# Rows turned for the router ahead of their norm, the norm's weight folded into the router matrix, and tile 0 placed one PSUM bank at a time

## The chip, the cores and the metric

The kernel runs on one core of one Trainium2 chip, in one launch. The metric is the device time of that launch in microseconds. It is a hybrid block of a network (a mixer of three branches, then a mixture of experts) in float32, written directly for the five engines, with every wait on a semaphore in the code.

## The reference

512 tokens of width 1024. What matters here is what follows the mixer:

```python
xn = rms_norm(x, norm1_g[l])
x = x + hybrid_mixer(xn, ...)            # ends with: merged @ w_out
xn = rms_norm(x, norm2_g[l])             # x * rsqrt(mean(x*x) + 1e-6) * g
x = x + hierarchical_moe(xn, ...)
...
return rms_norm(x, final_norm_g)

def hierarchical_moe(x, wg, bg, we, be, w_gate, w_up, w_down):
    g_logits = xt @ wg + bg              # 4 groups
    g_idx = argmax(g_logits)
    e_logits = (xt @ we + be) of the chosen group   # 4 of 16 experts
    top_p, top_i = lax.top_k(softmax(e_logits), 2)
    combine = g_w * top_p / sum(top_p)   # on the two experts chosen
    for e in range(16):
        h = silu(xt @ w_gate[e]) * (xt @ w_up[e])
        y = y + combine[:, e:e + 1] * (h @ w_down[e])
```

## The kernel before, in words

**Two-part arithmetic.** Every large product is made of three matmuls: each operand is split into a high part (ScalarE writes `w_hi`, `xT_hi`, ... as fp32r) and the rest (`w_lo`, `xT_lo`, ..., a subtraction on GpSimd or VectorE). A weight block is 128x1024 elements, 512 KB. Blocks are numbered `b`; four slots (`HI_SLOTS`) hold split blocks. `split_hi(b)` waits until TensorE is done with block `b - 4`; TensorE waits for `split_lo(b)` with `lo_wait`. On SyncE's queue the loads of the next blocks wait for `lo_wait` of the block whose buffer they take.

**The end of the mixer.** `merged @ w_out` is made in two column halves. The first half is four blocks (`B_OUT` to `B_OUT + 3`, 24 matmuls each). The second half, blocks `B_OUT + 4` to `B_OUT + 7`, goes by rows: for each of four row tiles `t` the 24 matmuls of all four blocks, so that row tile 0 is ready first. After a row tile (`x2_ps`) VectorE adds the residual (`x_rows`, semaphore `x2_done`), ScalarE squares and sums the row (`y_tile`, `x2_sq`), VectorE scales the sum, GpSimd takes the power -1/2 (`stat`), VectorE writes the normed rows `xn2`. TensorE turns `xn2` in eight transposes (`turn_xn2`), ScalarE copies the turned rows out of PSUM (`xn2T`), and TensorE multiplies them with the 20 columns of `router_w` (`logits`).

The loop on ScalarE which serves this part is the same before and after the change. Its order is what counts: the square of row tile `t` stands ahead of the copy of row tile `t - 1`.

```python
for t in range(NT + 1):
    if t < NT:
        act.wait_ge(S["x2_done"], NT + t + 1)
        ...activation(y_tile, x_rows[:, t, :], ACT.Square, ...)
    if 1 <= t <= NT:
        act.wait_ge(S["xn2T_ps"], t)
        ...activation(xn2T[:, (t - 1) % 2, :], ps[...], ACT.Copy)
```

Just ahead of that loop ScalarE splits the four blocks of the second half. Between `split_hi(B_OUT + 3)` and `split_hi(B_OUT + 4)` it issues six small loads on its own queue, among them the router matrix (`route_in`, `g2_in`).

**Routing.** VectorE turns the logits into two experts for each token in a chain of small operations on `route` (each `link` waits for the one before), gives TensorE the choice in bf16 (`picked`), which counts tokens per expert with triangular matrices, and computes a slot of the scratch table `slots` for each token. Tile 0 (the first 128 tokens of expert 0) is not read back from `slots`: VectorE writes a 0/1 matrix into `silu` (`tile0_where`) and TensorE places the rows with 32 float32 matmuls into two PSUM banks (`ps[:, 3:5]`). In the meantime GpSimd scatters `xn2` into `slots` with eight indirect DMAs (`scattered`), from which SyncE loads the rows of tiles 1, 2 and so on.

**Expert tiles.** A tile is twelve blocks: eight for gate and up, four for down of the tile before. 14 tiles stand in fixed order, the others come from a table. `on_pool` says which `split_lo` GpSimd makes: of the expert blocks only the first four of tile 0. `AHEAD = 3`: splits run three blocks ahead of TensorE. At the end GpSimd gathers the results from `slots` and VectorE weighs and norms them.

Of the kernel before, what the change touches and what calls it, by code (L numbers as in the profile page):

```python
# [26 lines left out]
ALU = mybir.AluOpType  # L27
# [54 lines left out]
def on_pool(r):  # L82

    return r < 4

LO_DVE_0 = 32


def pool_before(r):
    return sum(on_pool(x) for x in range(r))


def build(nc, a, out):
# [10 lines left out]
    with ctx:  # L106
# [70 lines left out]
        with ExitStack() as s2:  # L177
# [15 lines left out]
            sb(s2, "to_line", [P, 8])  # L193
# [32 lines left out]
        def y_hi(t):  # L226
# [16 lines left out]
            "tile0_where xn2T_ps xn2T_done logits_ps gexp_in gexp_done eexp_done picked counts_ps routed scattered tab "  # L243
# [61 lines left out]
        POOL_TILE = pool_before(8 + PER_TILE) - pool_before(8)  # L305
        DVE_TILE = PER_TILE - POOL_TILE

        def lo_wait(eng, b):

            if b < B_EXP:  # L310
                eng.wait_ge(S["lo_pool"], b + 1)
            elif on_pool(b - B_EXP):
                eng.wait_ge(S["lo_pool"], B_EXP + pool_before(b - B_EXP + 1))
            else:
                eng.wait_ge(S["lo_dve"], LO_DVE_0 + b - B_EXP + 1 - pool_before(b - B_EXP + 1))

        def lo_wait_loop(eng, i, r):

            tile = r // PER_TILE
            c = 8 + r % PER_TILE  # L320
            if on_pool(c):
                eng.wait_ge(S["lo_pool"], i * POOL_TILE + (B_EXP + pool_before(c + 1) + (tile - 1) * POOL_TILE))
            else:
                eng.wait_ge(S["lo_dve"],
                            i * DVE_TILE + (LO_DVE_0 + c + 1 - pool_before(c + 1) + (tile - 1) * DVE_TILE))
# [15 lines left out]
        def split_lo(eng, b):  # L341
# [4 lines left out]
               .then_inc(S["lo_pool"] if b < B_EXP or on_pool(b - B_EXP) else S["lo_dve"], 1)  # L346

        def split_lo_loop(eng, at, r):
# [3 lines left out]
               .then_inc(S["lo_pool"] if on_pool(8 + r) else S["lo_dve"], 1)  # L352
# [11 lines left out]
        def _(sp):  # L364
# [119 lines left out]
            for r in range(PER_TILE):  # L484
                if r == 3:

                    sp.wait_ge(S["scattered"], 16 * 2 * NT)
# [31 lines left out]
        def _(pool):  # L519
# [59 lines left out]
            for r in range(AHEAD):  # L579
                split_lo(pool, B_EXP + r)  # L580

# [8 lines left out]
            for r in range(AHEAD, 8 + AHEAD):  # L590
                if r < 8:
                    if on_pool(r):
                        split_lo(pool, B_EXP + r)
            for r in range(8, 8 + AHEAD):
                if on_pool(r):
                    split_lo_loop(pool, at_odd(0), r - 8)
            def tile(at):
                for r in range(PER_TILE):
# [1152 lines left out]
```

## Time and profile before

| | |
|---|---|
| Time, median of 3 runs | 869.72 us (869.38 to 871.4) |
| The profiled execution's own time | 869.15 us |
| Its span, first to last instruction | 867.4 us |
| TensorE busy | 801.0 us, 92% of the span |
| VectorE, ScalarE, GpSimd busy | 495.5, 449.2 and 218.0 us |
| Mean granted clock of TensorE | 0.965 of full |

A page of the profile gives busy times over the whole span. The change sits in some 90 us of it, so the useful views are the timelines of those stretches: each line has a start, a duration, the engine and source line, what is written from what, and in brackets how long the engine had been idle and who released it. A line with a count stands for several instructions of one kind in a row, from the first's start to the last's end. The granted clock is 1.00 for 2.4 GHz and 0.50 for 1.2 GHz.

### The profile page before, as it was taken

What the parts mean: (1) busy time and instruction counts of PE and PEld (TensorE: products, weight loads), DVE (VectorE), ACT (ScalarE), POOL (GpSimd) and SP (SyncE); (2) the same over time, 40 slices, a digit from 0 to 9 for tenths busy, and PEclk for the clock granted to TensorE, in tenths of its full rate; (3) what the DMA queues carried; (4) which work ended last, traced back from release to release, by engine and by line L of the source; (5) the groups of instructions that cost most, each with busy time, mean ns of one, the idle gap of its engine ahead of it and who ended that gap; (6) DMA issues with size and microseconds to landing.
All of it is one profiled execution on the core that took longest, in us unless ns stands there. A gap on an engine that the chain in (4) does not pass through costs nothing.

```text
span 867.4 us, 10612 instructions
## 1 busy us (share of the span) xinstructions
PE 801.0 (92%) x3635; PEld 631.7 (73%) x3635; DVE 495.5 (57%) x649; ACT 449.2 (52%) x580; POOL 218.0 (25%) x126
## 2 busy tenths in 40 slices
PE   4999999999979999999999967899999999999960
PEld 3887766676756888888888866688787787877750
DVE  6613647657472222204012435698889898988865
ACT  5244637454552232323222221687888878887842
POOL 5554323132232344444444234000000000000013
PEclk9999999999999999999999967999999999999995
DMA  8665451512120343333328364999999999975945
GB/s 308 179 243 188 128 194 49 194 49 74 40 80 27 89 169 118 99 93 95 98 96 280 131 239 197 366 400 385 405 389 393 408 395 406 389 299 209 367 137 207
DMA packets 126633, 186.76 MB, mean 215 GB/s; under 512 B 9149, under 2 KB 61957, under 8 KB 126597
## 3 DMA queue, kind: packets, MB, share of 16 engines
q1 hardware_dynamic: 119156, 167.82, 54.3%
q10 hardware_dynamic: 5136, 10.08, 3.1%
q0 software_dynamic: 2304, 8.39, 2.7%
q8 instruction: 22, 0.36, 0.2%
q14 instruction: 15, 0.11, 0.0%
HBM read 158.99 MB, written 27.28 MB: 215 GB/s over the span
## 4 chain that ended last, share of the span: by engine, by line
PE 81%; DVE 7%; ACT 4%; issue 3%; DMA 2%; POOL 1%; ACTq 1%; DVEq 0%; SPq 0%
PE ps L947 24%; PE ps L949 23%; PE ps L948 23%; PE ps L1030 3%; PE ps L1010 2%; PE ps L1171 2%; PE ps L1019 1%; DVE w_lo L350 1%; PE ps L1119 1%; ACT w_hi L339 1%; DVE rgate L1394 1%; PE ps L1178 1%; DMA x<-in_x 1%; ACT xn L879 1%; DMA slots<-y_tile 1%
## 5 line engine op out<-in xcount | busy, mean ns | idle before, releaser
L344 POOL TENSOR_TENSOR w_lo<-raw,w_hi 128x1024 fp32r<-128x1024 f32 x72 | 176.2, 2450 | 286.8 <-ACT w_hi L332 286.8
L332 ACT ACTIVATE w_hi<-raw 128x1024 fp32r<-128x1024 f32 x73 | 77.0, 1057 | 169.0 <-PE ps L949 159.9
L947 PE MATMUL ps<-xn_hi,w_hi 128*128 128x512 f32 x352 | 143.8, 409 | 0.0
L949 PE MATMUL ps<-xn_hi,w_lo 128*128 128x512 f32 x352 | 137.5, 390 | 0.0
L948 PE MATMUL ps<-xn_lo,w_hi 128*128 128x512 f32 x352 | 137.3, 390 | 0.0
L947 PE MATMUL ps<-w_hi,xT_hi 128*128 128x512 f32 x256 | 105.2, 411 | 8.1 <-DVE xT_lo L1644 5.5
L948 PE MATMUL ps<-w_lo,xT_hi 128*128 128x512 f32 x256 | 102.3, 399 | 0.0
L949 PE MATMUL ps<-w_hi,xT_lo 128*128 128x512 f32 x256 | 102.2, 399 | 0.0
L947 PEld LDWEIGHTS ps<-xn_hi,w_hi 128*128 128x128 f32 x352 | 66.0, 188 | 26.8 <-issue 13.8
L614 POOL DMA_INDIRECT raw_mg<-slots,slot_idx x7 | 6.9, 982 | 303.6 <-ACTq L930 295.1
L949 PEld LDWEIGHTS ps<-xn_hi,w_lo 128*128 128x128 f32 x352 | 66.1, 188 | 14.4
L948 PEld LDWEIGHTS ps<-xn_lo,w_hi 128*128 128x128 f32 x352 | 66.2, 188 | 13.1 <-issue 1.0
L350 DVE TENSOR_TENSOR w_lo<-raw_mg,w_hi 128x1024 fp32r<-128x1024 f32 x57 | 68.0, 1221 | 4.3 <-ACT w_hi L339 1.7
L947 PEld LDWEIGHTS ps<-w_hi,xT_hi 128*128 128x128 f32 x256 | 48.9, 191 | 24.2 <-DVE w_lo L350 8.0
L1457 DVE SCALAR_TENSOR_TENSOR macc<-raw,ps 128x512 f32<-128x512 f32 x16 | 11.0, 688 | 96.5 <-PE ps L949 96.3
L339 ACT ACTIVATE w_hi<-raw_mg 128x1024 fp32r<-128x1024 f32 x57 | 59.7, 1056 | 11.3 <-PE ps L949 11.3
L350 DVE TENSOR_TENSOR w_lo<-raw,w_hi 128x1024 fp32r<-128x1024 f32 x43 | 51.3, 1220 | 14.6 <-ACT w_hi L339 14.6
L949 PEld LDWEIGHTS ps<-w_hi,xT_lo 128*128 128x128 f32 x256 | 48.9, 191 | 11.7
L948 PEld LDWEIGHTS ps<-w_lo,xT_hi 128*128 128x128 f32 x256 | 48.9, 191 | 10.4
L947 PE MATMUL ps<-w_hi,hT_hi 128*128 128x512 f32 x128 | 51.8, 405 | 2.9 <-DVE hT_lo L1651 2.9
L339 ACT ACTIVATE w_hi<-raw 128x1024 fp32r<-128x1024 f32 x43 | 44.0, 1055 | 16.1 <-PE ps L949 16.1
L949 PE MATMUL ps<-w_hi,hT_lo 128*128 128x512 f32 x128 | 50.5, 395 | 0.0
(260 smaller groups left out, 1457.5 us busy)
## 6 DMA issues: line engine op xcount, KB each, us to landing
raw<-in_w_in SPq DMA_DIRECT2D x52, 512.0 KB, 3.7
raw_mg<-in_exp_w_down SPq DMA_DIRECT2D x36, 512.0 KB, 8.3
raw<-in_exp_w_gate SPq DMA_DIRECT2D x28, 512.0 KB, 10.3
raw_a<-in_exp_w_gate SPq DMA_DIRECT2D x27, 512.0 KB, 9.8
raw_c<-in_exp_w_up SPq DMA_DIRECT2D x27, 512.0 KB, 9.2
slots<-raw SPq DMA_DIRECT2D x24, 512.0 KB, 6.5
raw_mg<-in_exp_w_up SPq DMA_DIRECT2D x21, 512.0 KB, 9.8
raw<-in_exp_w_up SPq DMA_DIRECT2D x16, 512.0 KB, 9.5
```

What stands on the lines that cost most here:

```text
L332: nc.scalar.activation(w_hi[:, b % HI_SLOTS, :], raw_buf(b), ACT.Copy)\
L339: nc.scalar.activation(w_hi[:, (8 + r) % HI_SLOTS, :], buf, ACT.Copy).then_inc(S["hi_act"], 1)
L344: eng.tensor_tensor(w_lo[:, b % HI_SLOTS, :], raw_buf(b), w_hi[:, b % HI_SLOTS, :].bitcast(F32), ALU.subtract)\
L350: eng.tensor_tensor(w_lo[:, (8 + r) % HI_SLOTS, :], place(at, r)[0], w_hi[:, (8 + r) % HI_SLOTS, :].bitcast(F32), ALU.subtract)\
L879: act.activation(at.y, ps[:, 5:7, :].rearrange("p a n -> p (a n)"), ACT.Copy).then_inc(S["y_act"], 1)
L947: pe.matmul(dst, hi_l, hi_r, start=start, stop=False)
L948: pe.matmul(dst, hi_l, lo_r, start=False, stop=False)
L949: return pe.matmul(dst, lo_l, hi_r, start=False, stop=stop)
L1010: pe.matmul(ps[:, 4 + n % 2, 0:(i + 1) * P], qT[hp, jp % 2, i * P:(i + 1) * P], kT[hp, jp % 2, 0:(i + 1) * P], start=True, stop=True).then ...
L1030: mm = pe.matmul(ps[DH * h:DH * (h + 1), 7, i * P:(i + 1) * P], v_rows[:, kt, (2 * jp + h) * DH:(2 * jp + h + 1) * DH], probsT[:, kt * P:( ...
L1171: mm = pe.transpose(ps[:, 3 + k // 4, (k % 4) * P:(k % 4 + 1) * P], rows[:, k * P:(k + 1) * P], ident[:, :])
L1457: dve.scalar_tensor_tensor(out=macc[:, 1, :], in0=gate_buf[:, g % 3, :], scalar=1.0, in1=ps[:, 2 + c, :], op0=ALU.add, op1=ALU.mult)\
```

## The change

What it does, in the order of the kernel:

- ScalarE issues one more load, `g2_cols`: the 1024 values of `norm2_g` laid out with one row of eight on each partition. VectorE multiplies the router matrix with it once, ahead of the first row tile, after `g2_rows` (`g2_in`) and the six other loads of that group (`route_in` at 96) have landed.
- The router gets the rows as they are, ahead of their norm: `turn_x2(t - 1)` stands in the middle of row tile `t`'s matmuls and `logits(t - 1)` right behind them, one row tile earlier than before. VectorE multiplies the logits with the row's 1/rms afterwards and then adds the bias.
- In the routing chain the two subtractions that feed the exponentials move behind the choice; `picked_bf` is written by one addition; the table of tiles (`tables`) and the weights of the experts (`weights`) move behind tile 0's splits and behind the last tile.
- The 0/1 matrix is written in four parts, one for each 128 tokens, and TensorE fills bank 3 wholly ahead of bank 4. ScalarE and VectorE split each bank on its own, and the first two weight blocks need only the first half.
- All `split_lo` of expert blocks are VectorE's. Those of tile 0 stand behind the routing chain, where GpSimd made three of them during it.
- `xT_lo_part(2)` now stands ahead of `hidden`, with `tables` ahead of both.

The diff, cut to its core:

```diff
+                    act.dma_start(g2_cols[:, :], a["norm2_g"][0].rearrange("(k p) -> p k", p=P),
+                                  allow_slow_non_contiguous=True)\
+                       .then_inc(S["route_in"], 16)
                     act.dma_start(router_w[:, :, 0:NG], a["router_grp_w"][0].rearrange("(k p) n -> p k n", p=P))\
...
             dve.wait_ge(S["g2_in"], 16)
+            dve.wait_ge(S["route_in"], 96)
+            dve.tensor_tensor(router_w[:, :, :], router_w[:, :, :],
+                              g2_cols[:, :].unsqueeze(2).to_broadcast([P, KD, NG + NE]), ALU.mult)\
+               .then_inc(S["router_scaled"], 1)
...
-                if t >= 2:
-                    logits(t - 2)
+                    if kp == 1 and t >= 1:
+                        turn_x2(t - 1)
                 if t >= 1:
-                    turn_xn2(t - 1)
-            turn_xn2(NT - 1)
-            logits(NT - 2)
+                    logits(t - 1)
+            turn_x2(NT - 1)
             logits(NT - 1)
...
-            for r in range(AHEAD):
-                split_lo(pool, B_EXP + r)
...
-                              hid[:, 0:P].unsqueeze(1).to_broadcast([P, NT, P]), spread(slot0, NT, P),
-                              ALU.is_equal).then_inc(S["tile0_where"], 1)
+            for t in range(NT):
+                dve.tensor_scalar(silu[:, t * P:(t + 1) * P], hid[:, 0:P], slot0[:, t:t + 1], None, ALU.is_equal)\
+                   .then_inc(S["tile0_where"], 1)
...
-            xT_lo_part(1)
-            for r in range(AHEAD, 8):
-                if not on_pool(r):
-                    split_lo(dve, B_EXP + r)
+            for half in range(2):
+                split_lo(dve, B_EXP + half)
+                dve.wait_ge(S["tile0_hi"], half + 1)
+                dve.tensor_tensor(xT_lo[:, 4 * half:4 * half + 4, :].rearrange("p k n -> p (k n)"), ps[:, 3 + half, :],
+                                  xT_hi[:, 4 * half:4 * half + 4, :].rearrange("p k n -> p (k n)").bitcast(F32),
+                                  ALU.subtract).then_inc(S["tile0_lo"], 1)
+            dve.sem_inc(S["xT_done"], 1)
+            for r in range(2, 8):
+                split_lo(dve, B_EXP + r)
             for r in range(8, 8 + AHEAD):
-                if not on_pool(r):
-                    split_lo_loop(dve, at_odd(0), r - 8)
+                split_lo_loop(dve, at_odd(0), r - 8)
+            tables()
+            xT_lo_part(2)
             hidden(B_EXP + 8, 1)
-            xT_lo_part(2)
```

The first place is TensorE's row around the router's products. Before, this stands at the end of row tile 2: `logits(0)`, whose copy ScalarE made a row tile ago, then the turning of row tile 1.

```order
L949 MATMUL ps<-w_hi,mg_lo 128x512
L1119 MATMUL ps<-router_w,xn2T 128x20 [waits xn2T_done,route_in]
L1119 MATMUL ps<-router_w,xn2T 128x20 x7
L1128 MATMUL ps<-ident,xn 128x128 [waits xn2_done]
L1128 MATMUL ps<-ident,xn 128x128 x7
```

In the changed kernel this stands at the end of row tile 1: the last three matmuls of it, `logits(0)` right behind them, and then the first of row tile 2.

```order
L908 MATMUL ps<-w_hi,mg_hi 128x512
L909 MATMUL ps<-w_lo,mg_hi 128x512
L910 MATMUL ps<-w_hi,mg_lo 128x512
L1080 MATMUL ps<-router_w,xn2T 128x20 [waits xn2T_done,router_scaled]
L1080 MATMUL ps<-router_w,xn2T 128x20 x7
L908 MATMUL ps<-w_hi,mg_hi 128x512
```

The product for row tile 0 moved from behind the matmuls of row tile 2 to behind those of row tile 1, and waits for the copy `xn2T_done`.

The second place is ScalarE's row between the last product of the mixer and the router. Of before, from the last of the small loads on:

```order
L832 DMA gf_rows<-in_final_norm_g 128x1024
L332 ACTIVATE w_hi<-raw 128x1024 [waits w_used,raw_in0]
L332 ACTIVATE w_hi<-raw 128x1024 [waits w_used,raw_in1]
L332 ACTIVATE w_hi<-raw 128x1024 [waits w_used,raw_in2]
L332 ACTIVATE w_hi<-raw 128x1024 [waits w_used,raw_in3]
L841 ACTIVATE y_tile,stat<-x_rows 128x1024 [waits x2_done]
```

Of the changed kernel, the loads and then what stands behind the four splits (the splits themselves are as above):

```order
L777 DMA g_rows<-in_norm_g 128x1024
L778 DMA g_cols<-in_norm_g 128x8x1
L781 DMA router_w<-in_router_grp_w 128x8x4
L783 DMA router_w<-in_router_exp_w 128x8x16
L785 DMA router_b<-in_router_grp_b 128x4
L787 DMA router_b<-in_router_exp_b 128x16
L789 DMA gf_rows<-in_final_norm_g 128x1024
```

```order
L798 ACTIVATE y_tile,stat<-x_rows 128x1024 [waits x2_done]
L798 ACTIVATE y_tile,stat<-x_rows 128x1024 [waits x2_sq,x2_done]
L805 ACTIVATE xn2T<-ps 128x1024 [waits xn2T_ps]
L798 ACTIVATE y_tile,stat<-x_rows 128x1024 [waits x2_sq,x2_done]
L805 ACTIVATE xn2T<-ps 128x1024 [waits xn2T_ps]
```

One load of 128x8 single elements came in ahead of the router matrix; the order of squares (`y_tile`) and copies (`xn2T`) is that of before.

The third place is VectorE behind the slots of all tokens. In the changed kernel the splits of tile 0 follow directly, with the two halves of the rows between the first three:

```order
L1582 CAST slot_idx<-route 128x4
L323 TENSOR_TENSOR w_lo<-raw_a,w_hi 128x1024 [waits hi_act]
L1633 TENSOR_TENSOR xT_lo<-ps,xT_hi 128x512 [waits tile0_hi]
L323 TENSOR_TENSOR w_lo<-raw_a,w_hi 128x1024 [waits hi_act]
L1633 TENSOR_TENSOR xT_lo<-ps,xT_hi 128x512 [waits tile0_hi]
L323 TENSOR_TENSOR w_lo<-raw_a,w_hi 128x1024 [waits hi_act]
```

Before, the same stretch held the table and the weights, then the whole of the turned rows, and only splits from `raw_c` on: those from `raw_a` were GpSimd's.

```order
L1639 TENSOR_REDUCE w_first<-route 128x4 [waits dve_chain]
L1644 TENSOR_TENSOR xT_lo<-ps,xT_hi 128x1024 [waits xT_hi_done,dve_chain]
L344 TENSOR_TENSOR w_lo<-raw_c,w_hi 128x1024 [waits hi_act] x3
L344 TENSOR_TENSOR w_lo<-raw,w_hi 128x1024 [waits hi_act]
L350 TENSOR_TENSOR w_lo<-raw,w_hi 128x1024 [waits hi_act] x3
```

The three splits from `raw_a` moved from GpSimd, during the routing, to VectorE, behind it.

## Rows read from the trace of the kernel before

**Rows 1.** Timeline of PE at the end of row tile 1: start us, us, instruction.
```profile
487.56 0.39 PE L949 MATMUL ps<-w_hi,mg_lo 128*128 128x512 f32 x1
```

**Rows 2.** Timelines of DVE and ACT behind row tile 1.
```profile
487.99 0.69 DVE L1507 TENSOR_TENSOR x_rows<-ps,x_rows 128x512 f32<-128x512 f32 x1 [1.36 <-PE ps L949]
488.72 1.06 ACT L841 ACTIVATE y_tile<-x_rows 128x1024 f32<-128x1024 f32 x1 [4.22 <-DVE x_rows L1507]
...
489.78 1.01 ACT L848 ACTIVATE xn2T<-ps 128x1024 f32<-128x1024 f32 x1
```

**Rows 3.** Timeline from the mixer's last matmul to the last logits, PE.
```profile
502.21 1.85 PE L1119 MATMUL ps<-router_w,xn2T 128*128 128x20 f32 x16
...
506.47 1.97 PE L1128 MATMUL ps<-ident,xn 128*128 128x128 f32 x8 [1.49 <-DVE xn L1513]
...
508.23 6.86 PE L1119 MATMUL ps<-router_w,xn2T 128*128 128x20 f32 x32
```

**Rows 4.** Windows of PE: stretch, length, busy, granted clock, DMA share, GB/s.
```profile
506.40:515.20 8.80, 8.62 (x40) 0.50 0.87 305
...
553.90:557.20 3.30, 3.30 (x9) 0.50 1.01 359
```

**Rows 5.** Timeline of ACT: issues of small loads, and the split behind them.
```profile
460.07 0.45 ACTq L824 DMA_DIRECT2D router_w<-in_router_grp_w  x1
460.55 0.60 ACTq L826 DMA_DIRECT2D router_w<-in_router_exp_w  x1
461.18 6.61 ACTq L828 DMA_DIRECT2D router_b<-in_router_grp_b  x1
...
469.18 2.01 ACT L332 ACTIVATE w_hi<-raw 128x1024 fp32r<-128x1024 f32 x2 [8.88 <-issue]
```

**Rows 6.** DMA issues, 455 to 486 us: KB each, us from issue to landing.
```profile
gf_rows<-in_final_norm_g ACTq DMA_DIRECT2D x1, 512.0 KB, 11.8
router_w<-in_router_exp_w ACTq DMA_DIRECT2D x1, 64.0 KB, 16.5
router_w<-in_router_grp_w ACTq DMA_DIRECT2D x1, 16.0 KB, 11.2
```

**Rows 7.** Timeline of POOL: the `w_lo` of blocks `B_OUT + 4` to `B_OUT + 6`.
```profile
470.32 7.10 POOL L344 TENSOR_TENSOR w_lo<-raw,w_hi 128x1024 fp32r<-128x1024 f32 x3 [11.23 <-ACT w_hi L332]
```

**Rows 8.** Timeline of the routing chain.
```profile
510.52 6.98 POOL L344 TENSOR_TENSOR w_lo<-raw_a,w_hi 128x1024 fp32r<-128x1024 f32 x3 [5.42 <-ACT w_hi L332]
...
515.70 1.83 DVE L1558 TENSOR_TENSOR route<-route 128x16 f32<-128x16 f32 x1
...
523.07 0.69 DVE L1586 TENSOR_TENSOR silu<-hid,route 128x512 f32<-128x512 f32 x1
...
523.81 10.32 PE L1194 MATMUL ps<-silu,xn 128*128 128x128 f32 x64 [1.05 <-DVE silu L1586]
```

**Rows 9.** Timeline of SyncE's issues: start us, us, instruction.
```profile
515.19 2.71 SPq L377 DMA_DIRECT2D raw_a<-in_exp_w_gate  x3
542.04 0.82 SPq L461 DMA_DIRECT2D xn<-slots  x2
```

**Rows 10.** The instructions on `slots`, 520 to 560 us: min/median/max ns, first and last start.
```profile
L587 POOL DMA_INDIRECT slots<-xn,slot_idx x8: 951/955/1206, 528.6 to 537.7; - x8
...
DMA to landing us min/median/max: 3.6/4.4/5.4
```

**Rows 11.** Timeline of tile 0 and the start of tile 1.
```profile
536.82 0.80 PE L947 MATMUL ps<-w_hi,xT_hi 128*128 128x512 f32 x1 [2.68 <-DVE xT_lo L1644]
...
549.61 1.04 PE L1171 MATMUL ps<-ident,xn 128*128 128x128 f32 x8
...
551.64 0.68 DVE L1659 TENSOR_TENSOR hid<-silu,ps 128x512 f32<-128x512 f32 x1
552.24 1.22 DVE L1644 TENSOR_TENSOR xT_lo<-ps,xT_hi 128x1024 fp32r<-128x1024 f32 x1
553.51 0.53 PE L947 MATMUL ps<-w_hi,xT_hi 128*128 128x512 f32 x1 [2.87 <-DVE xT_lo L1644]
```

More of the change, by code:

```diff
@@ L192, in build @@
             router_b = sb(s2, "router_b", [P, NG + NE])
-            sb(s2, "to_line", [P, 8])
+            g2_cols = sb(s2, "g2_cols", [P, KD])
             xT_hi = sb(s2, "xT_hi", [P, KD, P], F32R)
@@ L1187, in expert_block @@
                 mm.then_inc(S["w_used"], 1)
[L1191 to L1192 removed]
+            for half in range(2):
                 for t in range(NT):
[L1194 to L1197 removed]
+                    if half == 0:
+                        pe.wait_ge(S["tile0_where"], t + 1)
+                    for k in range(4 * half, 4 * half + 4):
+                        mm = pe.matmul(ps[:, 3 + half, (k % 4) * P:(k % 4 + 1) * P], xn2[:, t, k * P:(k + 1) * P],
+                                       silu[:, t * P:(t + 1) * P], start=(t == 0 and k % 4 == 0),
+                                       stop=(t == NT - 1 and k % 4 == 3))
+                mm.then_inc(S["tile0_half"], 1)
+            pe.sem_inc(S["xT_ps"], 1)
             for r in range(8):
+                pe.wait_ge(S["tile0_lo"], 1 if r < 2 else 2)
                 lo_wait(pe, B_EXP + r)
@@ new lines, in weights @@
+            def weights():
+                dve.wait_ge(S["gexp_done"], 1)
+                comb = row(12, NT, NE)
+                dve.wait_ge(S["eexp_done"], 1)
+                link(dve.tensor_tensor(comb, comb, sel1, ALU.mult))
+                link(dve.tensor_reduce(e_sum, comb, AX.X, ALU.add))
+                link(dve.tensor_reduce(g_sum, row(4, NT, NG), AX.X, ALU.add))
+                link(dve.tensor_tensor(scale_t, g_sum, e_sum, ALU.mult))
+                link(dve.reciprocal(scale_t, scale_t))
+                link(dve.tensor_tensor(comb, comb, spread(scale_t, NT, NE), ALU.mult))
+                for k, s in enumerate((s_first, s_second)):
+                    link(dve.tensor_tensor(late, slot, spread(s, NT, NE), ALU.is_equal))
+                    link(dve.tensor_tensor(late, late, comb, ALU.mult))
+                    link(dve.tensor_reduce(w_first[:, k, :], late, AX.X, ALU.add))
@@ L1695, in _ @@
             hT_lo_part(tiles)
-            if not on_pool(8 + AHEAD):
-                split_lo_loop(dve, at_last(n_last), AHEAD)
+            split_lo_loop(dve, at_last(n_last), AHEAD)
+            weights()
             for t in range(NT):
```

129 lines of the change are left out of this document (39 added, 90 removed).

## The prediction

> **What bounds the kernel now.** I read the page first: TensorE is busy 92% of the span, so what the change can win or lose are the stretches in which TensorE waits or runs at 1.2 GHz. Then I read the timeline from the mixer's last product to tile 1, in order, asking at each gap of TensorE what came last.
>
> The first stretch is the second half of `merged @ w_out`. TensorE has no gap there. Its last matmul of row tile 1 starts at 487.56 [rows 1], so it is free for the next instruction at 487.79, and the last of row tile 3 is issued before 502.21 [rows 3]. Between these two lie two row tiles, one `logits` and two turnings. A `logits` at 1.2 GHz takes half of 6.86 us, 3.43, so 1.7 at 2.4 GHz; a turning takes 508.23 - 506.47 = 1.76, so 0.9 [rows 3]. What is left, 14.42 - 1.7 - 1.8 = 10.9 us for 48 matmuls, is 0.228 us each and 5.45 for a row tile.
>
> The second is the tail from 502.21 to the last logits at 515.09, 12.9 us. The reader is to see the wait on the norm (1.49 us idle) and that from 506.4 on the clock is 0.50 [rows 3, 4]: what TensorE did since 502.21 was one small product, a turning and that idle time.
>
> The third is the routing chain. One operation of VectorE, over 16 columns, takes 1.83 us [rows 8]. GpSimd is at a split until 510.52 + 6.98 = 517.50, and that is when it ends: VectorE was held by GpSimd. The chain's other small operations are about 0.22 us (22 of them and TensorE's count of 0.7 between 517.50 and 523.07).
>
> The fourth is the placement, 10.3 us from 523.81, then 2.7 us idle until 536.82, tile 0 until 549.61, and 2.87 us idle until tile 1 at 553.51 [rows 8, 11]. From 523.81 (call it X) to tile 1 it is 29.7 us. At 549.61 the turning of tile 1's rows starts with no wait, so the load of these rows, issued at 542.04 and 3.6 us under way [rows 9, 10], had some 4 us to spare.
>
> **The change, part by part.**
>
> *The added load.* `g2_cols` is 128x8 single values of 4 bytes, no two of which are neighbours both in DRAM and on their partition: 1024 pieces. ScalarE issues it between two splits that GpSimd and TensorE need. The issues there are not free: the fourth took 6.61 us with no semaphore in it, and the next split starts at 469.18, 8.9 us late [rows 5]. The router's two matrices are 1024 pieces each, of 16 and 64 bytes. They landed at 460.07 + 11.2 = 471.3 and 460.55 + 16.5 = 477.05 [rows 5, 6]: 5.8 us for 1024 pieces whether these are of 16 or 64 bytes. I read the 6.61 us as the queue being full: ScalarE goes on when so many pieces have drained. A third set of 1024 ahead of them then holds ScalarE 5.8 us longer, until 475.0. No row here shows such a load itself. The Trainium skill ("DMA: Bandwidth & Descriptors", Rules for kernel authors) says that a non-contiguous last dimension becomes one descriptor per element, which agrees with the count.
>
> What is late next: `w_lo` of `B_OUT + 4` to `B_OUT + 7`. The three first take 7.10 us, 2.37 each, and start 1.14 us behind the split's start [rows 5, 7]. So GpSimd would run from 476.1 and finish the fourth at 476.1 + 4 x 2.37 = 485.6. TensorE wants it for the last six matmuls of row tile 0, at 487.79 - 5.45 - 6 x 0.228 = 480.95. Loss: **+4.6 us**, spread over gaps of one to one and a half us between the four blocks. Bounds: 0 (the issue waits for something else), and 7 (pieces of 4 bytes drain more slowly). The same shift brings the last load from 468.49 + 11.8 = 480.3 [rows 6] to about 486. VectorE's multiplication of the matrix waits for that load, ahead of row tile 0's addition at about 487: hidden, by a us.
>
> *The router's products one row tile earlier.* This is the largest term. `logits(0)` now stands right behind row tile 1 and needs the copy of row tile 0. On ScalarE that copy stands behind the square of row tile 1, which needs VectorE's addition, which needs row tile 1's last matmul. The chain is in the trace: TensorE free at 487.79, addition 487.99, square 488.72, copy from 489.78 to 490.79 [rows 1, 2]. Before, nobody waited for it, since `logits(0)` came a row tile later. Now TensorE waits 490.84 - 487.79 = 3.05 us, behind row tile 1 and again behind row tile 2: **+6.1 us**. Queued behind the waiting product are all matmuls of the next row tile. The turnings have no such wait, their rows are added 2 us before. Besides, one `logits` and one turning move from the tail to ahead of the last row tile's end: **+2.5 us** there, counted off in the tail.
>
> *The clock.* TensorE's clock was at 0.50 for 3.3 us behind the 2.87 us of idle time at 553.51, with nine matmuls in it [rows 4, 11]; this costs half, 1.7. I take it behind both new gaps: **+3.4 us**. Bounds 0 and 6.
>
> *The tail.* From the last matmul of row tile 3: 3.05 us to the copy of row tile 2, `logits(2)`, turning, copy (1.1), `logits(3)`. At 2.4 GHz 3.05 + 1.7 + 0.9 + 1.1 + 1.7 = 8.4 us; at 1.2 GHz 3.05 + 3.43 + 1.76 + 1.1 + 3.43 = 12.8. Before, the clock fell 4 us into the tail with less idle time in it, so I take 12.0: **-0.9 us** against 12.9. `logits(2)` is queued ahead of a turning that could go first.
>
> *The routing chain.* GpSimd splits nothing during it, so the hold is gone: 1.83 becomes nothing at all, since that subtraction moves behind the choice. Added: the multiplication with 1/rms, 0.26. Removed ahead of `picked`: an addition (0.22) and a subtraction. In all -1.9. The 0/1 matrix's first quarter takes about 0.2 in place of 0.69 [rows 8]: -0.5. Sum **-2.4 us**; the slots of all tokens come 0.1 us later against that.
>
> *From X to tile 1.* Two paths end here. TensorE's: placement 10.3; tile 0 follows at once, as the first half is split during the second, so the gap of 2.7 and the slow start behind it (1.7) go: 12.8 - 1.7 = 11.1, end at X + 21.4. Then splits, the tables (seven operations, 1.5) in the place of `hid` (0.7), so 3.9 + 0.8: X + 26.1. The rows' path: eight scatters from X + 5.4 on, SyncE's load at 542.04 - 523.81 + 0.6 = X + 18.8. But three loads of 512 KB, which SyncE issued at 515.19, in quiet time [rows 9], now wait for VectorE's splits of blocks 0, 1 and 2, at about X + 6, X + 10 and X + 13, and SyncE's load of the rows stands behind them. The scatters themselves, 4.2 MB in some 10 us [rows 10], already fill the DMA engines (359 GB/s at a share of 1.01 [rows 4]). 1.6 MB more delay them by 3.5 us, some of 4.4 being ahead of them: X + 22.3, landed at X + 25.9, and turning, copy and split to tile 1 take 3.5: X + 29.4. The rows' path is last: **-0.3 us**. Bounds: -3.6 (loads cost nothing, TensorE's path) and +2.
>
> The weights of the experts at the end (twelve operations, some 2.6 us) lie in VectorE's wait for the gathered rows. The rest of the tiles is unchanged.
>
> **Sum.** 4.6 + 6.1 + 2.5 + 3.4 - 0.9 - 2.4 - 0.3 = +13.0 on 869.15, the profiled execution's own time: 882.2. The median of before lies 0.6 above that execution, so I say 882.5.
>
> **Rivals.**
>
> 1. *The issue costs nothing.* If the 6.61 us were no full queue, or 4-byte pieces drained quickly, the first term goes: 877.9. Against it: the same 5.8 us for two sizes. For it: no row shows the queue's limit.
> 2. *The clock holds at 2.4 GHz.* -3.4 and, in the tail, -3.6: 875.5. Against: it fell behind each gap over 1.4 us in these rows. With rival 1 as well: 870.9, no change that can be told.
> 3. *The seam shrinks, faster.* Place: from the last matmul of row tile 3 to tile 1, 51.3 us now. If TensorE's path, not the rows', sets tile 1 (the loads fit beside the scatters), and TensorE is at 2.4 GHz in the tail, the seam gives 4.5 + 2.4 + 3.6 = 10.5. That beats the 8.6 of moved work and stalls, so it decides once issue and clock together cost under 1.9: 867.8 with them at nothing, and 866 with the placement at 2.4 GHz too. Against: 4.2 MB of scatters fill the DMA engines alone.
> 4. *GpSimd is held by VectorE.* VectorE held by GpSimd is in rows 8; the other way round the eight descriptor writings, 0.95 us each [rows 10], would wait for splits of 1.2 us. Up to four of them: +5, 887.5. The Trainium skill ("SBUF — State Buffer", Who interferes with whom) has the shared port pair as an exclusive lock for a two-input operation against GpSimd's reads; whether writing descriptors counts, no row here shows, since VectorE had small operations only at that time.
>
> **Chances.** Sum as above 0.50, rival 1 0.18, rival 2 0.10, both 0.07, rival 3 0.08, rival 4 0.07. The range 870.5 to 887 leaves out rival 3 and some of rival 4. A measurement of this kernel tells about 0.3%, 2.6 us, from no change: faster than 867.1 0.08, within 0.10, slower 0.82.
>
> **What would show it.** ScalarE's first split behind the loads at about 475, with one issue of over 10 us in sum; TensorE's gaps of about one us inside row tile 0; gaps of 3.05 us before `router_w` products behind row tiles 1, 2 and 3, released by ScalarE's copy; the clock at 0.50 behind them; no operation over 0.3 us in the routing chain; no gap between placement and tile 0; and TensorE's longest gap of the stretch, some 7 us, before the turning of tile 1's rows, released by their load. The prediction is wrong if ScalarE is back at 469, if the products find their copy done, or if tile 1 starts under X + 27.

## The result, and the profile after

The changed kernel takes 890.16 us (median of 4, 889.05 to 891.39) against 870.21 us of the kernel before on the same chips (4 runs): a ratio of 1.0229, 95% interval 1.0209 to 1.0248. It is 20 us slower. The forecast had the sign, and 882.5 us; its range ended at 887.0. The profiled execution has 889.90 us and a span of 887.9 us, and it is typical for its kernel.

The forecast is the prediction's sum, stage by stage. The time is best told by milestones which both traces have: the addition of `x_rows` for the first half (F), for row tiles 0 and 3 (T0, T3), VectorE's first operation on the logits (L), TensorE's first placement matmul (X) and the first matmul of tile 1.

| stretch | before | after | difference | forecast |
|---|---|---|---|---|
| start to F | 477.18 | 480.32 | +3.14 | 0 |
| F to T0 (load issue) | 5.44 | 9.84 | +4.40 | +4.6 |
| T0 to T3 (products' waits, clock, moved work) | 19.78 | 33.71 | +13.93 | +12.0 |
| T3 to L (tail) | 12.82 | 13.07 | +0.25 | -0.9 |
| L to X (routing chain) | 8.59 | 6.29 | -2.30 | -2.4 |
| X to tile 1 | 29.70 | 30.71 | +1.01 | -0.3 |
| tile 1 to the end of the execution | 315.64 | 315.96 | +0.32 | 0 |

The load and the splits behind it, in timelines of the changed kernel (ACT, POOL, PE):

```profile
463.21 0.46 ACTq L778 DMA_DIRECT2D g_cols<-in_norm_g  x1
463.69 0.79 ACTq L781 DMA_DIRECT2D router_w<-in_router_grp_w  x1
464.51 6.37 ACTq L783 DMA_DIRECT2D router_w<-in_router_exp_w  x1
470.91 5.36 ACTq L785 DMA_DIRECT2D router_b<-in_router_grp_b  x1
...
477.80 3.90 ACT L311 ACTIVATE w_hi<-raw 128x1024 fp32r<-128x1024 f32 x4 [14.35 <-issue]
...
478.94 9.48 POOL L323 TENSOR_TENSOR w_lo<-raw,w_hi 128x1024 fp32r<-128x1024 f32 x4 [16.70 <-ACT w_hi L311]
...
481.37 0.50 PE L908 MATMUL ps<-w_hi,mg_hi 128*128 128x512 f32 x1 [1.16 <-POOL w_lo L323]
...
488.47 0.50 PE L908 MATMUL ps<-w_hi,mg_hi 128*128 128x512 f32 x1 [0.68 <-POOL w_lo L323]
```

The issues of `router_exp_w` and `router_grp_b` took 0.60 and 6.61 us [rows 5]; now they take 6.37 and 5.36, 4.5 us more in sum. ScalarE sits 14.35 us ahead of its first split instead of 8.88. GpSimd ends the fourth `w_lo` at 488.42 and TensorE waits for each of the four in turn, inside row tile 0. The stretch from F to T0, gap-free and 5.44 us long before, now takes 9.84. The row after that, and where the clock went (PE):

```profile
492.69 1.03 PE L1089 MATMUL ps<-ident,x_rows 128*128 128x128 f32 x8
...
499.42 3.57 PE L1080 MATMUL ps<-router_w,xn2T 128*128 128x20 f32 x16 [2.96 <-ACT xn2T L805]
502.82 0.77 PE L908 MATMUL ps<-w_hi,mg_hi 128*128 128x512 f32 x1
...
513.81 1.96 PE L1080 MATMUL ps<-router_w,xn2T 128*128 128x20 f32 x16 [2.87 <-ACT xn2T L805]
515.62 0.49 PE L908 MATMUL ps<-w_hi,mg_hi 128*128 128x512 f32 x1
...
526.71 3.60 PE L1080 MATMUL ps<-router_w,xn2T 128*128 128x20 f32 x16 [2.87 <-ACT xn2T L805]
530.14 1.95 PE L1089 MATMUL ps<-ident,x_rows 128*128 128x128 f32 x8
533.21 3.60 PE L1080 MATMUL ps<-router_w,xn2T 128*128 128x20 f32 x16 [1.11 <-ACT xn2T L805]
```

Three products of the router wait 2.96, 2.87 and 2.87 us for ScalarE's copy; the prediction had 3.05. ScalarE's rows show why (timeline of ACT of the changed kernel):

```profile
497.22 1.06 ACT L798 ACTIVATE y_tile<-x_rows 128x1024 f32<-128x1024 f32 x1 [5.18 <-DVE x_rows L1475]
...
498.27 1.00 ACT L805 ACTIVATE xn2T<-ps 128x1024 f32<-128x1024 f32 x1
```

The square of row tile 1 and the copy of row tile 0 follow each other exactly as in [rows 2], only that TensorE now stands and waits for the copy. Windows of PE in the changed kernel (columns as in [rows 4]) show the clock at 0.50 behind both gaps and in the tail, whose products take 3.60 us each, as at 1.2 GHz [rows 3]:

```profile
495.00:500.00 5.00, 2.04 (x10) 0.92 0.00 0
500.00:505.00 5.00, 5.00 (x20) 0.50 0.02 3
...
515.00:520.00 5.00, 5.00 (x19) 0.66 0.00 0
...
530.00:535.00 5.00, 3.89 (x19) 0.50 0.99 356
```

The stretch from the placement to tile 1, in timelines of the changed kernel (PE, POOL, DVE, SP) and one window of PE, answers to [rows 8 to 11]:

```profile
543.23 9.17 PE L1156 MATMUL ps<-silu,xn 128*128 128x128 f32 x64 [0.57 <-DVE silu L1554]
552.15 0.48 PE L908 MATMUL ps<-w_hi,xT_hi 128*128 128x512 f32 x1
...
569.60 1.97 PE L1131 MATMUL ps<-ident,xn 128*128 128x128 f32 x8 [5.89 <-DMA xn<-slots]
573.94 0.80 PE L908 MATMUL ps<-w_hi,xT_hi 128*128 128x512 f32 x1 [2.37 <-DVE xT_lo L1613]
...
548.76 1.23 POOL L564 DMA_INDIRECT slots<-xn,slot_idx  x1 [22.20 <-DVE slot_idx L1582]
550.30 1.84 POOL L564 DMA_INDIRECT slots<-xn,slot_idx  x1 [0.30 <-issue]
...
554.96 1.96 POOL L564 DMA_INDIRECT slots<-xn,slot_idx  x1 [0.30 <-issue]
...
561.76 0.95 POOL L564 DMA_INDIRECT slots<-xn,slot_idx  x1 [0.30 <-issue]
...
550.09 1.21 DVE L323 TENSOR_TENSOR w_lo<-raw_a,w_hi 128x1024 fp32r<-128x1024 f32 x1
...
554.88 4.62 DVE L323 TENSOR_TENSOR w_lo<-raw_c,w_hi 128x1024 fp32r<-128x1024 f32 x4
...
548.94 6.41 SPq L356 DMA_DIRECT2D raw_a<-in_exp_w_gate  x3
566.29 0.82 SPq L440 DMA_DIRECT2D xn<-slots  x2
...
555.00:560.00 5.00, 5.00 (x22) 1.00 1.02 409
```

The gap between placement and tile 0 is gone, as forecast, and TensorE gets nothing for it: it waits 5.89 us for the rows of tile 1 instead. GpSimd writes the descriptors of the eight scatters itself. Four of these writings take 1.84 to 1.97 us, where all were at 0.95 to 1.2 [rows 10]. At the same time the DMA engines are full: their share is 1.02 here, with SyncE's three weight loads beside the scatters.

### The profile page after: what moved, and what is told of

The parts are those of the page before. It is cut to its first block, busy times and chain, and to the rows that moved or that the text cites. A ratio compares the mean times of both kernels' runs of the same rounds, so it can differ in the third digit from the quotient of the medians.

```text
span 887.9 us, 10608 instructions
## 1 busy us (share of the span) xinstructions
PE 809.6 (91%) x3635; PEld 635.3 (72%) x3635; DVE 499.2 (56%) x659; ACT 448.6 (51%) x581; POOL 212.3 (24%) x122
## 4 chain that ended last, share of the span: by engine, by line
PE 77%; DVE 7%; ACT 4%; POOL 3%; DMA 3%; issue 3%; ACTq 2%; DVEq 0%; SPq 0%; POOLq 0%
PE ps L908 23%; PE ps L910 21%; PE ps L909 21%; PE ps L991 2%; PE ps L971 2%; PE ps L1131 2%; PE ps L1080 1%; PE ps L980 1%; POOL w_lo L323 1%; POOL slots L564 1%; DVE w_lo L329 1%; DVE rgate L1358 1%; ACT w_hi L318 1%; PE ps L1138 1%; ACTq L783 1%
```

## The experiments

Each kernel is the changed kernel with the edit shown, unless another base is named. Its time is compared with the kernel before on its own chip, so ratios, not times, are to be compared between experiments: median 869.29 us (13 runs) for the first four, 870.18 (26) for the next four, 870.78 (23) for the last two. The intervals are 95%.

### e1_pieces: the added load as 128 pieces

```diff
-    act.dma_start(g2_cols[:, :], a["norm2_g"][0].rearrange("(k p) -> p k", p=P),
-                  allow_slow_non_contiguous=True)
+    act.dma_start(g2_cols[:, :], a["norm2_g"][0].rearrange("(p k) -> p k", p=P))
```

The same 4 KB, now 32 bytes for each partition in one piece. The router matrix is multiplied with the right number of values, but in another order, so this kernel routes differently; its work is the same but for the load.

> One layout is changed in the changed kernel: the weights of the norm are loaded as 128 runs of 32 bytes in place of 1024 single values, so the router matrix is multiplied with the right number of values in another order (the output is another one, the work is the same but for the load). Theory, a full queue that drains by pieces: ScalarE is back at its splits some 5.8 us earlier, about 8.5 us behind the end of its mg_hi work as before the change in place of 14.4, the four gaps of TensorE in row tile 0 (together 4.5 us) go, and the time falls from 890.2 by 4 to 5 us to about 885.7. Rival, the queue counts loads (seven in place of six) or bytes: ScalarE comes back as late as with single values, time 889 to 891. The early shift of 3.1 us ahead of any edited instruction stays under a cause in the program and may go under one of chance.

Measured: 886.76 us (883.93 to 889.67), ratio 1.0197 (1.0155 to 1.0239). The interval overlaps with that of the changed kernel (1.0209 to 1.0248), so the time alone doesn't decide; the stages do. The load's stretch in the timeline of ACT of e1_pieces:

```profile
463.01 1.75 ACTq L782 DMA_DIRECT2D router_w<-in_router_exp_w  x1
464.78 6.00 ACTq L784 DMA_DIRECT2D router_b<-in_router_grp_b  x1
...
472.19 2.96 ACT L311 ACTIVATE w_hi<-raw 128x1024 fp32r<-128x1024 f32 x3 [9.96 <-issue]
```

These two issues take 7.75 us in place of 11.73, and F to T0 is 5.43 us, that of before: the four gaps are gone. The packets of ScalarE's queue (q10) between 455 and 500 us agree with the count of pieces. Of before, of the changed kernel and of e1_pieces:

```profile
q10 hardware_dynamic: 2656, 1.14, 10.9%
```
```profile
q10 hardware_dynamic: 3696, 1.15, 11.9%
```
```profile
q10 hardware_dynamic: 2800, 1.15, 10.0%
```

1040 more in the changed kernel, 144 more here: 1024 and 128 pieces, and 16 in both. The number of pieces holds ScalarE, not their 4 KB. The median is 3.4 us lower (2.8 by the ratios) where 4 to 5 were expected, and the profile gained hardly any, because T0 to T3 took 36.58 us here, 2.9 more than in the changed kernel: the clock was at 0.50 over all of 495 to 500 and 510 to 515. So what the two gaps cost in clock is not a fixed amount: it differs by 2.9 us between two profiles with the same order of work. In two of its four runs it took 884 us, in two 889.5.

### e2_copy_first: ScalarE copies ahead of squaring

```diff
 for t in range(NT + 1):
+    if 1 <= t <= NT:
+        ...copy of row tile t - 1
     if t < NT:
         ...square of row tile t
-    if 1 <= t <= NT:
-        ...copy of row tile t - 1
```

> The changed kernel with one edit: on ScalarE the copy of row tile t - 1 stands ahead of the square of row tile t. Theory, the router's products wait for a copy that is queued behind a square: the three waits of about 2.9 us before the router's products go, and with them the half clock behind two of them (5 us by the trace); in the tail logits(2) follows at once. 6.1 + 5.2 us in the rows and 5 to 8 us in the tail: 871 to 874 in all, the load's 4.5 us still in it. Rival, the products were late for their own sake (the turning in the middle of a row tile, the clock that would fall anyway): under 3 us are won, 887 or more.

Measured: 871.99 us (10 runs), ratio 1.0031 (1.0014 to 1.0048): by the ratios 17 us better than the changed kernel, by one block of six lines moved. PE's timeline of e2_copy_first, which answers to the fence of the router's products above:

```profile
494.59 1.85 PE L1080 MATMUL ps<-router_w,xn2T 128*128 128x20 f32 x16
496.29 0.49 PE L908 MATMUL ps<-w_hi,mg_hi 128*128 128x512 f32 x1
...
510.98 1.85 PE L1080 MATMUL ps<-router_w,xn2T 128*128 128x20 f32 x16
512.68 1.07 PE L1089 MATMUL ps<-ident,x_rows 128*128 128x128 f32 x8
514.87 3.60 PE L1080 MATMUL ps<-router_w,xn2T 128*128 128x20 f32 x16 [1.11 <-ACT xn2T L799]
```

No wait ahead of the first three products, and these at 2.4 GHz. T0 to T3 is 22.75 us. That splits the changed kernel's 33.71: 19.78 of before; 2.97 for the moved product and turning (forecast 2.5); and 10.96 which e2 takes away. Of these, the waits are 499.42 - 496.30 and 513.81 - 510.78 (a matmul frees TensorE 0.23 us after its start), 6.15 us; the rest, 4.81, is the clock: the product until 502.82 takes 3.40 instead of 1.70, the next twelve matmuls 4.32 and 4.43 instead of 2.87, and the second product 1.81. The tail fell from 13.07 to 7.43 us, since no wait of 3 us stands in it and only its last product runs at 1.2 GHz. F to T0 is still 9.80 us: the load's loss remains.

### e3_fill: the gap filled with useless matmuls

```diff
+                if t in (1, 2):
+                    for _ in range(12):
+                        pe.matmul(ps[:, 3, :], mg_hi[:, 0, 0:P], w(B_OUT + 4, 0)[:, 0:512], start=True, stop=True)
                 if t >= 1:
                     logits(t - 1)
```

Twelve matmuls into a bank that nobody reads at that time, 2.88 us, so that TensorE works instead of waiting and the copy is as late as in the changed kernel.

> The changed kernel with twelve matmuls without use behind row tile 1 and twelve behind row tile 2, into a PSUM bank that row tile 3 starts anew, so that TensorE works through 2.7 of the 3.05 us for which it would wait for the copy. The waits stay what they are, only the clock can change. Theory, the clock behind the two waits costs 5.2 us: the granted clock stays at 1.00 from row tile 1 to row tile 3 and the time falls to 885 to 886. Rival, the clock falls for another reason, the low activity of the router's products themselves: it falls all the same, and the time stays at 889 to 891.

Measured: 883.74 us (878.99 to 885.18), ratio 1.0154 (1.0116 to 1.0192). The time is below the 885 to 886 that were expected, and the one profile has 885.18. Behind the filling the products still wait 0.25 and 0.16 us, and T0 to T3 is 28.99 us, 4.72 less than in the changed kernel: the clock's part by itself, beside 4.81 by the count above. Windows of PE of e3_fill:

```profile
495.00:500.00 5.00, 4.75 (x26) 1.00 0.00 0
500.00:505.00 5.00, 5.00 (x32) 1.00 0.02 3
505.00:510.00 5.00, 5.00 (x23) 1.00 0.00 0
```

So the low clock there needs the gap: the router's small products alone don't bring it, for they stand here too, and the clock is full.

### e4_before_again: the kernel before, profiled a second time

> The kernel before, unchanged, for a second profile. The changed kernel was 1.4 us late from 27 us on and 3.1 us late from 161 us on, ahead of its first edited instruction, with a granted clock of 0.59 near 20 us and 0.67 near 152 us where before had 1.00. Theory, chance of the execution: this profile shows such drops too, at one of these places or another, or its time differs by 1 to 3 us from the first. Rival, a lasting effect of the changed program: this profile has 1.00 at both places again, within 0.3 us of the first up to 455 us.

No edit; it asks whether the +3.14 us ahead of F belongs to the change. One execution, 872.24 us: F is at 478.54 us, 1.36 later than in the first profile, and the stretches from F to tile 1 are 5.44, 19.79, 12.81, 8.55 and 29.48 us, those of before within 0.25. Tile 1 to the end takes 317.63 us, 1.99 more. So two profiles of one kernel differ by 3.1 us, outside the stretches from F to tile 1. F is at 478.63 to 480.06 in the profiles of the other kernels here, whose first 460 us are not edited. A part of the shift ahead of F is thus the execution's.

### e5_cheap_load: e2, with a cheap layout for the load

A layout in which the load is 128 pieces and the routing is that of the reference: partition p holds features 8p to 8p + 7, so the router matrix is loaded in that order too and TensorE turns every eighth column of the row.

```diff
-    ...rearrange("(k p) -> p k", p=P), allow_slow_non_contiguous=True)
+    ...rearrange("(p k) -> p k", p=P))
... (router_grp_w as router_exp_w)
-    ...a["router_exp_w"][0].rearrange("(k p) n -> p k n", p=P))
+    ...a["router_exp_w"][0].rearrange("(p k) n -> p k n", p=P))
...
-    x_rows[:, t, k * P:(k + 1) * P], ident[:, :])
+    x_rows[:, t, :].rearrange("p (q k) -> p k q", k=KD)[:, k, :], ident[:, :])
```

> The kernel with the copy first (2.7 us above before), and the weights of the norm loaded as 128 runs of 32 bytes with the right result: feature 8p + k goes to partition p, the router matrix is loaded in the same order, and TensorE turns every eighth column. Theory, the single values held ScalarE 5.8 us and cost TensorE 4.5 us: the gaps in row tile 0 go, 4 to 5 us less, about 1.5 to 2 us under before. Rival, what is won there is lost in the turnings with a step of eight (they take more than 0.8 us each) or in the wait for the rows of tile 1: under 2 us less.

Measured: 867.80 us (866.48 to 868.31, 5 runs), ratio 0.9967 (0.9953 to 0.9981). F to T0 is 5.37 us, and T0 to T3 with 22.78 us shows that a turning of every eighth column costs TensorE nothing. With both stalls of the changed kernel mended, it is 0.3% faster than the kernel before.

### e6_pool_splits: e2, with the first three splits of tile 0 on GpSimd again

```diff
+            for r in range(AHEAD):
+                split_lo(pool, B_EXP + r)
...
             for half in range(2):
-                split_lo(dve, B_EXP + half)
...
-            for r in range(2, 8):
+            for r in range(3, 8):
```

The semaphores of these three splits go with them. With the splits done early, SyncE's three weight loads go out ahead of the scatters too, so two things change at once behind the placement.

> The kernel with the copy first, and the splits of tile 0's first three blocks on GpSimd again, ahead of the scatters, as before the change. Theory, these three splits on VectorE hold GpSimd's descriptor writing (four of eight took 1.8 to 2.0 us in place of 0.95) and bring three loads of 512 KB beside the scatters: at least the second and third descriptor writing get short again, the three loads go out before the scatters, and the rows of tile 1 land 2 to 4 us sooner behind the slots; against that VectorE is held once more in the routing chain, up to 2 us. Net -2 to 0. Rival, only the five later splits matter for the descriptors: the writings stay long, the wait for the rows of tile 1 stays at 6 to 7 us and the time is the same or 1 to 2 us more.

Measured: 871.79 us (10 runs), ratio 1.0009 (0.9991 to 1.0028), not told apart from e2 (1.0031), by two effects of opposite sign. Timelines of e6_pool_splits, DVE and POOL:

```profile
518.91 1.72 DVE L1525 TENSOR_TENSOR route<-route,router_b 128x80 f32<-128x80 f32 x1
520.67 0.17 DVE L1529 TENSOR_REDUCE route<-route 128x4 f32<-128x16 f32 x1
520.88 1.99 DVE L1508 TENSOR_TENSOR route<-route 128x16 f32<-128x16 f32 x1
...
515.87 6.97 POOL L323 TENSOR_TENSOR w_lo<-raw_a,w_hi 128x1024 fp32r<-128x1024 f32 x3 [1.97 <-ACT w_hi L311]
...
539.04 1.83 POOL L567 DMA_INDIRECT slots<-xn,slot_idx  x1 [0.30 <-issue]
```

GpSimd's splits hold the chain at two operations, L to X is 9.58 us instead of 6.27. In return seven of eight writings are back at 0.95 to 1.21, and X to tile 1 is 26.77 us instead of 31.60. The writings end at X + 16.4 instead of X + 19.2, and SyncE's load of the rows follows 2.96 us behind them instead of 4.32.

### e7_rows_first: e2, with the rows of tile 1 ahead of three weight loads on SyncE

```diff
-                if r == 3:
+                if r == 0:
                     ...loads of xn from slots
```

> The kernel with the copy first, and SyncE's two loads of rows from the slots issued ahead of the three weight loads that wait for splits 0 to 2, not behind them. The three loads then no longer run beside the scatters. Theory, the DMA engines are full with the scatters: the rows land 3 us sooner and the time falls by 2 to 3 us. Rival, the held descriptor writing sets the scatters' end, not the DMA engines: the last writing ends as late as before, the rows land within 1 us of before, the time is the same.

Measured: 870.17 us (10 runs), ratio 1.0010 (0.9993 to 1.0027), not told apart from e2 either. In its profile SyncE's load of the rows is issued 2.39 us behind the last writing instead of 4.32, the wait for the rows is 3.9 us instead of 7.1, and X to tile 1 is 28.96 instead of 31.60. The writings are held as in e2 and end at X + 19.17, as late as there.

### e8_no_row_turn: the row part undone, routing chain and tile 0 as changed

```diff
-                    if kp == 1 and t >= 1:
-                        turn_x2(t - 1)
+                if t >= 2:
+                    logits(t - 2)
                 if t >= 1:
-                    logits(t - 1)
+                    turn_x2(t - 1)
...
-                    act.dma_start(g2_cols[:, :], ...
```

The multiplications of the router matrix and of the logits are undone with it, and `turn_x2` turns the normed rows.

> The changed kernel without its row part: rows normed ahead of the turning, the router's products where they were before, no load of single values and no multiplication; the shorter routing chain, the placement by banks, the splits on VectorE and the late tables stay. By the stages of the two traces: chain -2.6, from the placement to tile 1 +1 to +2, all else as before: 0 to 1.6 us under before. Rival, that the chain's gain is given back wholly at the rows of tile 1: the same time as before or more.

Measured: 870.49 us (10 runs), ratio 0.9998 (0.9981 to 1.0015): the rest of the change by itself is worth nothing that can be told, where up to 1.6 us of gain were expected. In the profile L to X is 6.00 us, 2.59 less than before, and X to tile 1 30.33, 0.63 more. All 20 us come with the row part.

### e9_both and e10_fill_tile1

e9_both is e5_cheap_load with e7's order on SyncE. e10 adds sixteen useless matmuls behind tile 0, to keep the clock until the rows of tile 1 are there:

```diff
+            for _ in range(16):
+                pe.matmul(ps[:, 7, 0:P], ident[:, :], ident[:, :], start=True, stop=True)
             turn_x(x_odd, S["x_odd_in"], 16)
```

> The three mends together: copy ahead of square, the norm's weights as 128 runs, and the loads of rows ahead of the three weight loads. If the terms add, 4.5 us (load) and 1.8 us (rows) under the kernel with the copy first alone, which is 2 to 3 us above before: 3.5 to 4.5 us under before, a ratio of 0.995 to 0.996. If the rows' loads are worth nothing once the rest is earlier, the ratio stays at 0.997.

> The kernel with the three mends, and sixteen matmuls without use behind tile 0, which fill some 3.5 of the 4 us for which TensorE waits for the rows of tile 1. Theory, the clock at 0.50 behind that wait costs 1.7 us: it stays at 1.00 there and the time falls by 1 to 2 us. Rival, turning, copy and split behind the rows' landing (3.9 us, 2.4 of them idle) take the clock down all the same: no change.

Measured: e9_both 866.21 us (861.99 to 870.01, 12 runs), ratio 0.9949 (0.9926 to 0.9972): faster than both kernels, and as expected, though not told apart from e5. But its profile doesn't show the gain of e7: X to tile 1 is 31.63 us, as in e5 (31.66). The rows' load is issued 3.70 us behind the last writing instead of 5.04, but four writings are held instead of three, and the last ends at X + 19.6 instead of X + 18.6. Window of PE of e9_both, with the same columns as above:

```profile
535.00:540.00 5.00, 5.00 (x24) 1.00 0.59 237
```

The DMA engines are at 0.59 there, while GpSimd's writings are being held until 538.1: here the held writings alone delay the load. What this profile has less than that of e5 lies in the tail (5.83 instead of 7.13 us, since the last product of the router ran at 2.4 GHz this time behind the same wait of 1.11 us) and behind tile 1.

e10_fill_tile1 has 867.00 us, ratio 0.9964 (0.9943 to 0.9985), nothing gained. Timeline and windows of PE of e10_fill_tile1:

```profile
541.11 3.74 PE L1165 MATMUL ps<-ident 128*128 128x128 f32 x32
547.24 1.09 PE L1130 MATMUL ps<-ident,xn 128*128 128x128 f32 x8 [2.39 <-DMA xn<-slots]
550.70 0.79 PE L907 MATMUL ps<-w_hi,xT_hi 128*128 128x512 f32 x1 [2.37 <-DVE xT_lo L1614]
```
```profile
545.00:550.00 5.00, 1.09 (x8) 0.88 0.96 360
550.00:555.00 5.00, 4.30 (x10) 0.50 1.05 399
```

The turning ran in 1.09 us instead of the 1.97 of e9, so the filling kept the clock that far. But two more waits of 2.4 us follow, one ahead of the turning and one for `xT_lo`, and tile 1 starts at 1.2 GHz as before. From the turning to tile 1 it is 3.46 us here, 4.34 in e9 and in the changed kernel.

## Why the prediction was right in sign and short in size

**The added load: right.** Forecast +4.6, measured +4.40. The issue was held by the count of pieces, which e1_pieces shows by changing the pieces and not the bytes; rival 1 is out. ScalarE came back to its splits 5.5 us later behind its first issue (14.98 instead of 9.50 us), where 5.8 were forecast. The Trainium skill ("DMA: Bandwidth & Descriptors", Rules for kernel authors) has one descriptor per element for such a load, and the packets agree, 1024 more against 128. That every 1024 pieces take 5.8 us, whatever their size, is not shown: [rows 5, 6] have one distance between two landings, not one for each size, and in the changed kernel the three sets landed at 474.4, 480.2 and 481.5 us (the issues above, and 11.2, 16.5 and 17.0 us from issue to landing), 5.8 and 1.3 us apart.

**The products' wait for the copy: right.** Forecast 6.1, measured 6.15, and e2_copy_first removes it by the order on ScalarE alone.

**The clock: right in kind, too small.** The prediction took half of 3.3 us behind each gap, from one stretch of nine matmuls [rows 4]. Shown by e2 and e3 is 4.8 us in sum, and rival 2, the clock holds, is out. Behind the second gap it was 1.67 us, as in the model; behind the first it was 3.15, for there the product of the router ran at 1.2 GHz too, 3.40 us instead of 1.70. The row that was used as a model had no such product. The moved work was 2.97 instead of 2.5.

**The tail: wrong by 1.15.** The prediction worked out 12.8 us for a tail at 1.2 GHz throughout, and then took 12.0. The clock was lost within the wait of 2.87 us ahead of `logits(2)`, which took 3.60 us, so the full figure was right: 13.07.

**The routing chain: right.** -2.30 against -2.4; no operation of it ahead of the 0/1 matrix takes over 0.24 us, and e6 shows the hold by GpSimd come back when its splits do.

**X to tile 1: the path was right, the near hit in part luck.** The rows end last, as forecast, so rival 3 is out; tile 1 starts at X + 30.71 instead of X + 29.4. The load of the rows was issued at X + 23.07, forecast X + 22.3, and turning, copy and split took 4.34 us instead of 3.5, since the turning ran at 1.2 GHz (1.97 us; at 2.4 GHz in e10_fill_tile1 the three take 3.46). The prediction put the rows' delay down to 1.6 MB of loads that SyncE issues among the scatters. Its rival 4, GpSimd held by VectorE, had a chance of 0.07 as a case of its own, and it happened: the eight writings take 13.95 us from the first start to the last end, against 10.01 before, so they end at X + 19.5 instead of X + 14.8. Every long writing starts within a split of VectorE, as 550.30 and 554.96 do within the splits of 550.09 and 554.88, and ends 0.8 us behind that split's end. In e6 four writings are ahead of all splits, three start within 0.15 us of a split's edge, and the one that starts inside is the long one.

Yet the DMA engines were full in the same microseconds (a share of 1.02 from 555 to 560), as the prediction had it. The experiments part the two in one direction. With the weight loads out of the way and the writings held, the rows' load is issued at X + 21.56 (e7) and X + 23.31 (e9), instead of X + 23.52 (e2) and X + 23.64 (e5). With both out of the way, but for one held writing, it is X + 19.37 (e6), and before it was X + 18.23. So held writings alone are enough for most of the delay, and the prediction's X + 22.3 came near it without them. What the weight loads add differs between e7 and e9, and what they would cost beside writings that nobody holds was not run: both stay open.

**The step that failed** is the price of the clock, which was put too low in three places: 3.4 us behind the two gaps, 12.0 us for the tail, and tile 1's turning taken at 2.4 GHz. The runs showed 1.4, 1.15 and 0.8 us more, together 3.4 us over the forecast. All three are of one kind. Behind a wait stood small products or a turning, and they ran at 1.2 GHz; the row that was used as a model has large matmuls there. Misses of one kind add, and the range did not let them: the prediction's own upper bounds (7 for the load, 6 for the clock, 12.8 for the tail, +2 from X to tile 1) would have given 890.6 us together, and the range ended at 887. The other terms are 0.9 us over the forecast in sum: 0.5 for the moved work, 0.5 for the rows, which landed at X + 26.4 instead of X + 25.9, and -0.1 for the rest. That gives 886.8, still just inside the range.

The median is 3.4 us above this sum, and for that the runs show no cause. The profile has 3.14 us ahead of any edit. There it is the clock again: in the window from 150 to 155 us it is 0.66 in the changed kernel's profile and 1.00 in that of before, and 0.87 against 1.00 from 20 to 25. But the second profile of before has 0.76 from 150 to 155 and 1.36 us of such a shift. And e8 has 0.66 and 0.91 at these places and F at 480.06, and equals the kernel before in its median. So the shift is no proven cost of the change. The clock's price behind the gaps differs too, by 2.9 us between the profiles of e1 and of the changed kernel, and may be higher in the runs that were not profiled; that is not shown. Four runs of the changed kernel lie within 2.4 us, and why its median and not only its profile is 3.4 us above the sum of the terms stays open.

## What to carry to other kernels

When work moves one stage earlier on the engine that is the bound, look at every other engine's order in the same loop: here the product was moved and its feeder was not, and one moved block on ScalarE took back 17 of the 20 us. The price of the added load on the engine that issues it was its number of pieces, not its bytes, so a layout that makes a small vector contiguous on each partition is worth changing the order of a whole contraction, if the other operand can be read in that order for nothing. And a wait of 3 us on TensorE should be priced at nearly twice its length if small products follow it, since the clock goes with it: 6.15 us of waits cost 4.8 of clock in the changed kernel's profile. Bounds that have one cause in common are to be added. A number that comes out nearly right doesn't prove its reason: the rows' load was forecast to 0.8 us with a delay of the writings left out that took 3.9.

## What the runs showed of the hardware

- A descriptor writing of GpSimd that starts 0.07 us or more behind the start of a VectorE subtraction of 1.2 us with both inputs in SBUF, and 0.5 us or more ahead of its end, ends 0.8 us behind the subtraction's end: it takes 1.35 to 1.97 us instead of 0.95, in all profiles with such splits. One that starts only 0.02 to 0.03 us behind the subtraction's start was not held in seven of eight cases; there the subtraction took 1.28 instead of 1.21. A subtraction of 1.23 us with one input in PSUM held none (535.53 in the kernel before, over writings at 535.17 and 536.43; this is the one long operation of VectorE beside the writings there, which the prediction overlooked). The Trainium skill ("SBUF — State Buffer", Who interferes with whom) says that a VectorE instruction with two SBUF inputs contends with GpSimd's reads, and infers that descriptor generation is not touched by it; the measurement here speaks against the inference. The writing also reads `slot_idx` from SBUF, and which of its accesses is held isn't told apart.
- In the other direction VectorE is held until a split of GpSimd ends: 1.72 and 1.99 us for operations that take 0.24 and 0.17 alone, from 518.91 to 520.64 and from 520.88 to 522.87, beside splits that end at 520.54 and 522.83 (e6_pool_splits).
- 1024 more pieces of 4 bytes cost 4.5 us of issue on ScalarE, and 128 more of 32 bytes 0.5, beside two loads of 1024 pieces each.
- The granted clock fell to 0.50 twice within a wait of 2.9 to 3.0 us, ahead of 499.42 and of 526.71, and once 2.5 us behind such a wait, at about 516.3, with large matmuls under way. It did not fall at the first two gaps, those behind row tiles 1 and 2, when twelve useless matmuls stood there, which left waits of 0.25 and 0.16 us. Behind a wait of 1.11 us the last product of the router ran at 1.2 GHz in e2_copy_first (3.60 us) and at 2.4 GHz in e9_both (1.96 us).
